# A decoder layer on one core: part of a residual's transposes moved from TensorE to a DRAM round trip and VectorE

## The reference

```
x   = x + concat(RMSNorm(o_A), RMSNorm(o_B)) @ W_out
x   = x + MemCrossAttn(RMSNorm(x), RMSNorm(mem))          # 4 heads into 256 memory tokens
x   = x + HierMoE(RMSNorm(x))                             # top-1 group, then top-2 in group

q = (h @ w_q).reshape(b, s, MEM_HEADS, MEM_HEAD_DIM)      # memory queries, h = RMSNorm(x)
```

## Time and profile before

| what | value |
|---|---|
| median of three runs | 1356.27 us (1355.04 to 1357.63) |
| the profiled execution: its time, its span | 1355.84 us, 1354.1 us |
| TensorE busy | 998.5 us (74%) |
| VectorE busy | 579.0 us (43%) |
| ScalarE busy | 300.4 us (22%) |
| DMA | 486.40 MB, mean 359 GB/s |

### The profile page before, as it was taken

How to read it: one execution, slowest core, us unless ns; L and a number is a source line. 1 busy time by engine, 2 the same in 40 slices (tenths; PEclk the granted TensorE clock), 3 DMA queues, 4 the chain that set the end, 5 groups by cost and what they waited for, 6 DMA issues and landing times.

```text
span 1354.1 us, 20680 instructions
## 1 busy us (share of the span) xinstructions
PE 998.5 (74%) x8540; PEld 600.2 (44%) x8540; DVE 579.0 (43%) x1114; ACT 300.4 (22%) x521; POOL 52.4 (4%) x108
## 2 busy tenths in 40 slices
PE   8999999999999985666655566655566654566656
PEld 7888898888888532222212222222222221222222
DVE  5555566886657543223332233332223332223324
ACT  5554457674455100000000000000000000000002
POOL 1300001231000000000000000000000000000001
PEclk9999999999999998778787787787777877777878
DMA  7778763448869999999999999999999999999997
GB/s 247 263 238 255 217 167 123 144 136 273 286 252 338 358 417 428 433 430 432 433 430 434 432 432 434 433 429 433 429 434 432 433 433 433 430 432 430 433 426 303
DMA packets 78020, 486.40 MB, mean 359 GB/s; under 512 B 9943, under 2 KB 25437, under 8 KB 64798
## 3 DMA queue, kind: packets, MB, share of 16 engines
q1 hardware_dynamic: 77484, 483.46, 88.7%
q10 hardware_dynamic: 306, 2.11, 0.4%
q0 software_dynamic: 192, 0.31, 0.2%
HBM read 481.14 MB, written 4.72 MB: 359 GB/s over the span
## 4 chain that ended last, share of the span: by engine, by line
PE 51%; DMA 46%; SPq 1%; DVE 1%; issue 1%; ACT 0%; DVEq 0%; ACTq 0%
DMA gu<-in_w_up 42%; PE ps L1052 10%; PE ps L605 8%; PE ps L607 8%; PE ps L606 8%; PE ps L1107 5%; DMA down<-in_w_down 4%; PE ps L1031 2%; PE ps L1064 1%; PE ps L585 1%; PE ps L850 1%; PE ps L851 1%; PE ps L852 1%; PE ps L778 1%; SPq L470 0%
## 5 line engine op out<-in xcount | busy, mean ns | idle before, releaser
L1052 PE MATMUL ps<-gu,xe 128*32 128x256 f32 x3968 | 286.3, 452 | 306.0 <-DMA gu<-in_w_up 305.5
L2138 DVE TENSOR_TENSOR x_sum<-ps,x_sum 128x512 f32<-128x512 f32 x240 | 149.1, 684 | 507.6 <-PE ps L1064 507.6
L1052 PEld LDWEIGHTS ps<-gu,xe 128*32 128x32 f32 x3968 | 140.5, 129 | 469.3 <-DMA gu<-in_w_up 328.7
L1616 DVE TENSOR_TENSOR w_lo<-w_raw,w_hi 128x1024 fp32r<-128x1024 f32 (+1 forms) x137 | 164.6, 1208 | 118.1 <-ACT w_hi L1225 114.8
L605 PE MATMUL ps<-w_hi,a_hi 128*128 128x512 f32 (+1 forms) x468 | 183.4, 392 | 0.0
L606 PE MATMUL ps<-w_lo,a_hi 128*128 128x512 f32 (+1 forms) x468 | 179.7, 384 | 0.0
L607 PE MATMUL ps<-w_hi,a_lo 128*128 128x512 f32 (+1 forms) x460 | 176.8, 384 | 0.0
L1225 ACT ACTIVATE w_hi<-w_raw 128x1024 fp32r<-128x1024 f32 (+1 forms) x137 | 141.8, 1039 | 127.1 <-PE ps L607 88.6
L1535 ACT ACTIVATE sg<-ps 128x128 f32<-128x128 f32 x31 | 8.6, 278 | 654.3 <-PE ps L1052 654.3
L1107 PE MATMUL ps<-down,act_t 128*32 128x512 f32 x976 | 112.8, 603 | 5.3 <-DMA down<-in_w_down 5.3
L606 PEld LDWEIGHTS ps<-w_lo,a_hi 128*128 128x128 f32 x468 | 88.0, 188 | 16.4
(11 more groups left out here) (341 smaller groups left out, 854.9 us busy)
## 6 DMA issues: line engine op xcount, KB each, us to landing
down<-in_w_down SPq DMA_DIRECT2D x29, 4096.0 KB, 22.7
gu<-in_w_gate SPq DMA_DIRECT2D x28, 4096.0 KB, 31.7
gu<-in_w_up SPq DMA_DIRECT2D x28, 4096.0 KB, 41.0
w_raw<-in_w_in SPq DMA_DIRECT2D x56, 512.0 KB, 4.9
w_raw<-in_w_out SPq DMA_DIRECT2D x32, 512.0 KB, 4.7
gu<-in_w_up SPq DMA_DIRECT2D x18, 512.0 KB, 6.6
w_raw<-in_w_mem_kv SPq DMA_DIRECT2D x16, 512.0 KB, 3.5
down<-in_w_down SPq DMA_DIRECT2D x13, 512.0 KB, 15.5
```

The costliest lines, as they stand in the source:

```text
L1052: mm = pe.matmul(ps[5][j * SLOTS:(j + 1) * SLOTS, 0:2 * P].rearrange("s (m f) -> s m f", m=2), xe[:, k, :], gu[side][:, :, k, j * P:(j + 1 ...
L1616: ve.tensor_tensor(w_lo[:, u % RING, :, 0:n], w_raw[:, u % RING, :, 0:n], w_hi[:, u % RING, :, 0:n], ALU.subtract).then_inc(S("w_split"), 1)
L2138: ins = ve.tensor_tensor(x_sum[:, t, cols], ps[g][:, :], (x_res if first else x_sum)[:, t, cols], ALU.add)
```

## The change

Quarters 0 to 2 of the residual are no longer turned by TensorE. They join the list `QUADS`, so SP writes each to the scratch, waits, and reads it back into `nat[:, 0]`; VectorE transposes it there in two instructions; ScalarE and VectorE make `a2_hi` and `a2_lo` from SBUF. Since a 32 by 32 transpose leaves another order of features on the partitions, the rows of `w_mem_q` (six of its eight units, two DMAs each where one was) and the gains `norm_mem_x` (four small DMAs where one was) are loaded in that order. The fourth quarter stays on TensorE, and so does its code.

```diff
-QUADS = [SB_Q, SB_Q + 1, SB_K, SB_K + 1, MEM_K]
+QUADS = [SB_Q, SB_Q + 1, SB_K, SB_K + 1, MEM_K, W_OUT + 1, W_OUT + 3, W_OUT + 5]
 MOVE_AT = [DONE[_c] + RING + 3 for _c in QUADS]
+X_MOVED = QUADS.index(W_OUT + 1)
+X_QUADS = len(QUADS) - X_MOVED
...
+            if c == MEM_Q and by_quads(c, i):
+                q, b = divmod(i, UK)
+                return [w_mem_q[0, q * UN:(q + 1) * UN, :].rearrange(
+                    "(q k r) n -> k q r n", q=NJ, r=QUAD)[b * UK:(b + 1) * UK]]
...
                 c = QUADS[n]
                 sp.wait_ge(*chunk_out(c))
-                sp.dma_start(spill[n].rearrange("(t p) f -> p t f", p=P), nat[:, NAT[c]]).then_inc(
+                src = nat[:, NAT[c]] if n < X_MOVED else x_res[:, :, (n - X_MOVED) * UN:(n - X_MOVED + 1) * UN]
+                sp.dma_start(spill[n].rearrange("(t p) f -> p t f", p=P), src).then_inc(
                     S("spilled"), 16)
                 sp.wait_ge(S("spilled"), 16 * (n + 1))
                 if c == MEM_K:
                     sp.wait_ge(S("turned"), bank0[MEM_Q])
+                elif n >= X_MOVED:
+                    sp.wait_ge(S("split_lo"), SPLIT0["memx"] + 4 * (n - X_MOVED))
                 elif n >= 2:
...
             for q in range(1, D // UN):
                 project(W_OUT + 2 * q)
-                pe.wait_ge(*chunk_out(W_OUT + 2 * q - 1))
-                if q == 1:
-                    pe.wait_ge(S("sums_made"), 1)
-                split_turn("memx", x_res, 4 * (q - 1), 4 * q)
                 project(W_OUT + 2 * q + 1, a0=HEADS)
...
             def memx_heads(q):
 
-                split_head("memx", 32, hi=a2_hi, k_from=4 * q, k_to=4 * q + 4)
+                if q == X_QUADS:
+                    split_head("memx", 32, hi=a2_hi, k_from=4 * q, k_to=4 * q + 4)
+                else:
+                    for k in range(4 * q, 4 * q + 4):
+                        sc.wait_ge(S("split_turned"), (SPLIT0["memx"] + k) // 2 + 1)
+                        sc.activation(a2_hi[:, k, :].rearrange("p (j s) -> p j s", s=QUAD),
+                                      quads_of(X_MOVED + q)[:, :, k % 4 * QUAD:(k % 4 + 1) * QUAD], ACT.Copy,
+                                      scale=g_t[:, 32 + k:33 + k]).then_inc(S("split_hi"), 1)
                 x_squares(q, junk1)
...
+            def memx_turn(q):
+
+                ve.wait_ge(S("quads_loaded"), 16 * NJ * (X_MOVED + q + 1))
+                for b in range(2):
+                    tile = quads_of(X_MOVED + q)[:, :, b * UK * QUAD:(b + 1) * UK * QUAD]
+                    ve.transpose(tile, tile).then_inc(S("split_turned"), 1)
...
             for c in range(W_OUT, MEM_Q):
                 split_w(DONE[c] + RING - (1 if c == W_OUT else 0))
+                if c > W_OUT and (c - W_OUT) % 2 == 0:
+                    memx_turn((c - W_OUT) // 2 - 1)
                 add_heads(c)
```

More of the change, by code:

```diff
@@ L113 @@
         _b = len(SPLIT_BANK)
-        SPLIT_BANK.append(6 + _b % 2 if _name == "mem" else 4 + _b % 4)
+        SPLIT_BANK.append(None if _name == "memx" and _i < UK * X_QUADS else
+                          6 + _b % 2 if _name == "mem" else 4 + _b % 4)
 def bank_before(b):
@@ L276, in quads_of, with by_quads @@
         def quads_of(n):
-            if QUADS[n] == MEM_K:
-                return nat[:, 1].rearrange("p t (j f) -> p (t j) f", f=P)
+            if QUADS[n] >= MEM_K:
+                return nat[:, 1 if n < X_MOVED else 0].rearrange("p t (j f) -> p (t j) f", f=P)
             return quads[:, n % 2]
         first_turns = [ps[4][:, 0:SEQ], ps[2][:, 0:SEQ]]
+        def by_quads(c, i):
+            return c == MEM_Q and i < UK * X_QUADS
         def unit_src(c, i):
@@ L368, in load_small @@
             def load_small():
-                for gain, r0, rows in ((norm_mem_src, 16, 16), (norm_mem_x, 32, 16),
+                for gain, r0, rows in ((norm_mem_src, 16, 16),
                                        (norm_q_lat, 48, 4), (norm_kv_lat, 52, 2), (norm_mla_out, 54, 8),
@@ L374, in load_small @@
                                  ).then_inc(S("gains_loaded"), 16)
+                for q in range(NJ):
+                    rows = norm_mem_x[0, q * UN:(q + 1) * UN]
+                    sp.dma_start(g_nat[32 + 4 * q:36 + 4 * q, :], rows.rearrange("(k p) -> k p", p=P) if q >= X_QUADS
+                                 else rows.rearrange("(q k r) -> k q r", q=NJ, r=QUAD)).then_inc(
+                                     S("gains_loaded"), 16)
                 for t in range(TT):
@@ L451, in _ @@
                 (src,) = unit_src(c, i)
-                if len(src.shape) == 4:
+                if by_quads(c, i):
+                    for k in range(UK):
+                        sp.dma_start(dst[:, k, :], src[k]).then_inc(S(f"w_loaded{u % RING}"), 16)
+                elif len(src.shape) == 4:
                     for k in range(UK):
@@ L692, in _ @@
                 if i == 3:
-                    pe.wait_ge(S("gains_loaded"), 7 * 16)
+                    pe.wait_ge(S("gains_loaded"), (6 + NJ) * 16)
                     pe.transpose(ps[3][:, 0:86], g_nat[:, :], ident[0:86, 0:86]).then_inc(
@@ L835, in _ @@
             pe.wait_ge(*chunk_out(MEM_Q - 1))
+            pe.wait_ge(S("sums_made"), 1)
             split_turn("memx", x_res, KD - 4, KD)
@@ L867, in mem_scores @@
                 pe.wait_ge(S("turn_copied"), bank0[MEM_Q] + t + 1)
-                pe.wait_ge(S("quads_turned"), len(QUADS))
+                pe.wait_ge(S("quads_turned"), X_MOVED)
                 for p in range(2):
@@ L1459, in _ @@
             sc.wait_ge(S("rstd"), 6)
-            sc.wait_ge(S("quads_turned"), len(QUADS))
+            sc.wait_ge(S("quads_turned"), X_MOVED)
             sc.wait_ge(S("queries_made"), 1)
@@ L1860, in x_sums @@
                                  chunk_ss[:, :, :], AX, ALU.add).then_inc(S("sums_made"), 1)
-            def memx_rests(q):
-                split_rest("memx", 32, hi=a2_hi, lo=a2_lo, k_from=4 * q, k_to=4 * q + 4)
+            def memx_turn(q):
[3 more added lines that the diff above has]
+                    ve.transpose(tile, tile).then_inc(S("split_turned"), 1)
+            def memx_rests(q):
+                if q == X_QUADS:
+                    split_rest("memx", 32, hi=a2_hi, lo=a2_lo, k_from=4 * q, k_to=4 * q + 4)
+                    return
+                for k in range(4 * q, 4 * q + 4):
+                    ve.wait_ge(S("split_hi"), SPLIT0["memx"] + k + 1)
+                    ve.scalar_tensor_tensor(
+                        out=a2_lo[:, k, :].rearrange("p (j s) -> p j s", s=QUAD),
+                        in0=quads_of(X_MOVED + q)[:, :, k % 4 * QUAD:(k % 4 + 1) * QUAD],
+                        scalar=g_t[:, 32 + k:33 + k],
+                        in1=a2_hi[:, k, :].rearrange("p (j s) -> p j s", s=QUAD), op0=ALU.mult,
+                        op1=ALU.subtract).then_inc(S("split_lo"), 1)
             ve.wait_ge(S("rstd"), 5)
```

## The result

The changed kernel takes **1385.85 us** (median of four runs, 1385.18 to 1387.68), the kernel before 1356.49 beside it: a ratio of 1.0219, interval 1.0201 to 1.0237, or 29.4 us slower. The profiled execution took 1385.18 us.

The account below looks back on a forecast made before the run. It took the full expert-weight stream, started by the end of the memory queries, as the bound: -2.65 + 0.5 + 0.7 + 0.7 = -0.75 us, 1355.84 to 1355.1, plus 0.43 for the median, 1355.5; range 1353.2 to 1359.4 us.

Parts of the forecast that it names:

- Twelve half loads for six units of `w_mem_q`: Small edit behind quarter 2: the half loads add 6 x 0.4 us on SP and cost nothing.
- four rivals: Round trip hidden (0.24), DMA queue the bound (0.25), saving not reaching the end (0.05), more saved (0.04).
- What bounds the kernel: A microsecond TensorE gains or loses before the memory queries end moves the weight stream and the end by about one.
- TensorE sheds 2.65 us: Three turns of eight transposes leave TensorE's path at 0.88 us each, 2.65 us in all.
- the 6.6 us: Worth of the 24 transposes at the skill's 275 ns each; rival of more saved, 1349.7 to 1353, chance 0.04.
- Round trip of quarter 0: Write in DRAM at 326.4 us, data back at 330.7, TensorE waiting 0.5 us at `W_OUT + 4`.
- The sum of the Trainium skill: About 2.0 us plus bytes over 436 GB/s a DMA, 3.2 us for 0.5 MB; quarter 0 back by 324.7.
- Quarters 1 and 2 at 0.7 us each: DMA queue work of 13x + 4.3 = 22.5 us against 21.78 of matmuls; TensorE waits 0.7 us in each.
- The DMA queue becomes the bound: Rival: at 1.49 us a piece, two or three quarters end 1.9 us later each; 1357.9 to 1359.4, chance 0.25.
- x = 1.40: Time in us to move one 0.524 MB piece through a full DMA queue, chosen over 1.30 and 1.49.
- a DMA share near 0.95: Sign that the forecast is right: DMA engines' busy share near 0.95 from 318 to 375 us.
- The three added gain DMAs cost nothing: They put off the fifth unit's load by about a microsecond, at some 10 us, yet it lands no later.

Follow-up runs that it names:

- f3: f1 without any round trip: VectorE turns the three quarters straight out of `x_res`, so the queries' values change; 1355.57 us, 0.9989 against the kernel before.
- f4: The kernel before with the three round trips added on SP at the change's places, read into an unused tile; 1359.51 us, 1.0020.
- g1: f1 with VectorE's turns, heads and rests one `W_OUT` chunk later, and TensorE's wait for quarter 2 later; 1362.87 us, 1.0046 against before.
- g2: g1 with SP's wait for the spill and the four reads three weight units later; 1358.35 us, 1.0015 against before.
- e3: The changed kernel with its two half loads a unit in natural row order, slowest dimension 128; 1361.32 us, 1.0035 against before.
- e4: The changed kernel with each half load cut into two DMAs of slowest dimension 2, row order kept; 1414.92 us, one run.
- h1: The changed kernel with another feature order, VectorE turning every fourth column, so a `w_mem_q` unit is one copy; 1362.74 us, 1.0050 against before.
- h2: h1 with turns, heads and rests one chunk later and reads three weight units after the spill; 1357.70 us, 1.0011 against before.
- f1: The changed kernel with each of the six permuted `w_mem_q` units loaded by four 32-row copies instead of two; 1363.12 us, 1.0050 against before.

## Why the prediction was wrong

It forecast 1355.5 us and 68% for no change; the result lies 26 us above its range.

**The step that failed** is "Twelve half loads for six units of `w_mem_q` add 6 x 0.4 us on SP behind quarter 2, where the reads no longer press." It counted issues and took each half load to be half of a whole one. Its form was not looked at: with a slowest dimension of 4 it moves 102 GB/s, a half load needs 2.5 us for 0.26 MB, and a unit 5 us where TensorE needs one in 2.8. Even the issue was mis-sized, with a median of 2.4 us in place of 0.4. That is about the time in which one half load moves, so SP seems to be held up by the copies ahead. Price: 24.5 us in the changed kernel, 18.7 us alone. None of the four rivals held it; the working never asked what a weight load costs in its new form, because none of the rows showed one like it.

The other steps, by the trace after and f3, f4, g1 and g2:

- *What bounds the kernel*: right. The first memory scores and the span moved together, within 1 us in eleven of the thirteen kernels (e3: +4.1 and +5.0; e4: +59.4 and +59.1) and within 2.3 in all (after: +31.1 and +29.3).
- *TensorE sheds 2.65 us*: 2.5 by f3. Right; the 6.6 us worked out there from the Trainium skill (TensorE: Matmul & The Clock Gate, Part 4: PE-mode transpose) are not borne out.
- *Round trip of quarter 0*: right in its steps, and lucky in the clock time. The write was forecast in DRAM at 326.4 us and the chain has it there at 326.52, but it was issued at 319.43 instead of 318.3 and took 7.1 us instead of 8.1. (The sum of the Trainium skill that the prediction set against its own, DMA: Bandwidth & Descriptors, Anatomy of one DMA, is given there for copies that GpSimd issues; it makes 3.2 us of this write.) TensorE's wait was 0.27 us for 0.5. VectorE stands 2.55 us (forecast 2.9), and two transposes take 1.30 us (forecast 0.62 to 0.70 each):

```profile
331.52 1.30 DVE L1893 STREAM_TRANSPOSE nat<-nat 128x512 f32<-128x512 f32 x2 [2.55 <-DMA nat<-spill]
355.39 1.30 DVE L1893 STREAM_TRANSPOSE nat<-nat 128x512 f32<-128x512 f32 x2 [3.48 <-DMA nat<-spill]
379.77 1.30 DVE L1893 STREAM_TRANSPOSE nat<-nat 128x512 f32<-128x512 f32 x2 [3.02 <-DMA nat<-spill]
```

- *Quarters 1 and 2 at 0.7 us each*: too small. The change has 1.86 us at `W_OUT + 6`, and e3, with quick loads, shows

```profile
360.67 0.47 PE L625 MATMUL ps<-w_hi,a_hi 128*128 128x512 f32 x1 [1.45 <-DVE w_lo L1640]
```

```profile
384.84 0.47 PE L625 MATMUL ps<-w_hi,a_hi 128*128 128x512 f32 x1 [2.16 <-DVE w_lo L1640]
```

  That is the rival "The DMA queue becomes the bound", with its 1.9 us a quarter. The working took x = 1.40, from eight microseconds of a full queue, where the mean over the stage, 1.49, was the better price: e3's engines were busy 0.86 of the time from 318 to 375 us and moved 306 GB/s, which is 1.47 us for 0.524 MB. But the queue was not full. The forecast's sign, a DMA share near 0.95, failed: the share is no larger than before, 0.87, since it falls to 0.62 around the reads (326.5 to 331 us). In g2, where SP does not stand, it is 0.97, and TensorE has no wait in this stretch (windows of before, e3 and g2):

```profile
318.00:375.00 57.00, 57.00 (x265) 47.47 (x264) 36.03 (x41) 29.63 (x45) 0.00 (x0) 1.00 0.87 305
318.00:375.00 57.00, 55.29 (x243) 45.23 (x242) 37.37 (x43) 27.09 (x36) 0.00 (x0) 1.00 0.86 306
318.00:375.00 57.00, 57.00 (x254) 47.18 (x253) 39.42 (x46) 27.71 (x37) 0.00 (x0) 1.00 0.97 325
```

  The stage of e3 follows: 0.26 + 1.45 + 2.16 less 2.5 is 1.4 us, and the granted clock of 0.83 from 380 to 390 us, behind the longest wait, takes up to 1.7 more; 3.4 were measured.
- *The three added gain DMAs cost nothing*: not settled. The stage begins at 305.6 to 307.1 us in the kernels with the change's or later gain loads, at 305.2 to 305.5 in the three without. Against the loads as the cause speak h1 and h2: they load the gains at the program's start as before, and begin latest. The last section has what differs there.

With the form of the loads right, the rival "DMA queue becomes the bound" would have been nearest: it gave 1357.9 to 1359.4, and e3 and f1 took 1361.3 and 1363.1. The clock behind the waits, which the prediction has no term for, is up to 1.7 us of the rest in e3.

## What to carry to other kernels

When a change permutes rows, look at the access pattern of each DMA that loads them, not at its bytes: here a slowest dimension of 4 gave 102 GB/s and one of 2 gave 51, with the queue looking idle. A wait by the one engine that issues loads costs what is queued behind it; a later place for the second half of a round trip gave 4.5 us, while moving the consumer alone gave none (the later reads need the later consumer, too). And price every edit of a change by a row, above all those that look like bookkeeping.

## What the runs showed of the hardware

- SP's issue time grew where the copies ran at 102 GB/s: a half load took 0.56 us to issue at best and 3.56 at most, against a median of 0.43 for one of 128 rows in e3.
- The four reads of a trip landed in a median of 2.6 us in f1, where SP stands ahead of them and few loads run beside them, and in 6.2 us in g2, on the same queue with the loads going on.
- Copies to 32 partitions were slower with every engine busy. From 376 to 390 us the queue is full in f1 (four copies of 32 rows a unit) and in e3 (halves of 128 rows), at 256 and 336 GB/s. DMA views of f1 and then e3:

```profile
DMA packets 2312, 3.59 MB, mean 256 GB/s; under 512 B 340, under 2 KB 976, under 8 KB 2312
## 3 DMA queue, kind: packets, MB, share of 16 engines
q1 hardware_dynamic: 2312, 3.59, 101.1%
```

```profile
DMA packets 2848, 4.71 MB, mean 336 GB/s; under 512 B 271, under 2 KB 1031, under 8 KB 2848
## 3 DMA queue, kind: packets, MB, share of 16 engines
q1 hardware_dynamic: 2848, 4.71, 97.7%
```

  The Trainium skill (SBUF — State Buffer, Door 1: The DMA port swizzle) says that partitions 32 apart share ports, so that 32 neighbours reach half of the 16. The two rates agree in sign; early pieces of other forms are mixed into both, so no run here gives the factor by itself.
- The same first matmuls of the program run 0.23 us apart in some executions and 0.42 us apart in others for up to 2.3 us. The changed kernel's profiled execution has the close spacing from 11.2 us on, f4's from 8.4. TensorE's idle time just before does not tell them apart: 1.55 us there, 1.43 in f4. This shifts an execution by up to 1.3 us (the transposes that follow start between 11.28 and 12.60 us) whatever the change does later, and is why the stage, not the span, is compared above.
